# One inference step of a hybrid encoder on one core: VectorE's waits for itself, the spreading of expert ids, and the one-hot tables

## What is computed

```python
x = x + concat([sparse_attention(h), retention(h)]) @ w_out     # h = rmsnorm(x)
x = x + peer(rmsnorm(x));  y = rmsnorm(x)

def peer(h, w_query, keys1, keys2, exp_u, exp_v):               # 8 heads, 128 keys, 16384 experts
    q = (h @ w_query).reshape(T, 8, 2, 128)
    v1, i1 = top_k(q[:, :, 0] @ keys1.T, 16);  v2, i2 = top_k(q[:, :, 1] @ keys2.T, 16)
    cand_s = v1[..., :, None] + v2[..., None, :]                # 256 candidates per head
    top_s, sel = top_k(cand_s, 16);  e_idx = (i1 * 128 + i2)[sel]
    gate = softmax(top_s)
    act = gelu(einsum('thkd,td->thk', exp_u[e_idx], h))
    return einsum('thk,thkd->td', gate * act, exp_v[e_idx])
```

## Time and profile before

| | |
|---|---|
| median of 3 runs | 1158.07 us (1157.69 to 1158.08) |
| profiled execution, its own time | 1156.52 us |
| span of the profile | 1154.5 us |
| busy: PE, DVE, ACT, POOL | 873.4, 816.6, 448.7, 544.4 us |
| mean granted TensorE clock | 0.882 of full |
| bytes moved | 458.68 MB, 397 GB/s over the span |
| chain that ended last | DMA 43%, PE 25%, DVE 17%, POOL 6%, issue 5% |

### The profile page before, as it was taken

One profiled execution on the slowest core, in us unless ns is written; L12 is line 12 of the kernel. 1 busy time (PEld: TensorE's weight loads), 2 busy tenths in 40 slices (PEclk: granted clock), 3 DMA queues, 4 the chain that ended last, 5 costly groups with the idle time before them and its releaser, 6 DMA issues.

```text
span 1154.5 us, 12183 instructions
## 1 busy us (share of the span) xinstructions
PE 873.4 (76%) x3735; PEld 396.8 (34%) x3740; DVE 816.6 (71%) x2123; ACT 448.7 (39%) x1413; POOL 544.4 (47%) x437
## 2 busy tenths in 40 slices
PE   8999988997897957765766769587666756656566
PEld 6748743443333424232233333133222212211111
DVE  2325887876687889996867785757887777777544
ACT  2121444343444434433554663343333333333334
POOL 0002445553554645554553563545574555556442
PEclk9999999999998879787899898798988698887769
DMA  9902999999999999999999999999999999999995
GB/s 377 402 1 72 423 425 425 426 426 430 423 390 425 422 429 425 382 424 425 427 426 424 425 427 427 427 426 428 426 424 426 427 426 427 427 423 418 426 426 226
DMA packets 67079, 458.68 MB, mean 397 GB/s; under 512 B 8387, under 2 KB 10179, under 8 KB 15686
## 3 DMA queue, kind: packets, MB, share of 16 engines
q0 software_dynamic: 55888, 402.68, 83.2%
q1 hardware_dynamic: 10982, 54.97, 11.7%
q10 hardware_dynamic: 144, 0.26, 0.1%
HBM read 453.59 MB, written 3.24 MB: 396 GB/s over the span
## 4 chain that ended last, share of the span: by engine, by line
DMA 43%; PE 25%; DVE 17%; POOL 6%; issue 5%; ACT 3%; SPq 0%; POOLq 0%; DVEq 0%
DMA rows<-in_uv,ids 32%; PE ps L596 25%; DMA wt<-in_uv,ids 8%; DVE rows L2007 7%; POOL rows L535 3%; POOL work L518 2%; DMA rows<-in_w_qi 1%; DMA wt<-in_uv,last_ids 1%; DMA wt<-in_w_q 1%; DVE wt L2007 1%; DVE top L1596 1%; ACT work L1227 1%; DVE wt L1600 1%; ACT wt L1227 1%; POOL wt L535 1%
## 5 line engine op out<-in xcount | busy, mean ns | idle before, releaser
L535 POOL DMA_INDIRECT rows<-in_uv,ids x352 | 407.5, 1158 | 447.6 <-PE ps L596 360.4
L596 PE MATMUL ps<-rows,work 128*64 128x512 f32 x1416 | 419.5, 722 | 236.0 <-ACT work L1227 235.8
L2007 DVE CUSTOM_DVE_ANT_0 rows<-rows,wt 128x1024 f32<-128x1024 f32 x226 | 276.9, 1226 | 150.7 <-DMA rows<-in_uv,ids 147.5
L1227 ACT ACTIVATE zact<-zdot 128x1 f32<-128x1 f32 x354 | 71.5, 202 | 510.1 <-DVE zdot L2007 509.9
L596 PEld LDWEIGHTS ps<-rows,work 128*64 128x64 f32 x1416 | 97.4, 154 | 475.2 <-ACT work L1227 329.4
L596 PE MATMUL ps<-wt 128*128 128x128 f32 (+6 forms) x719 | 195.6, 478 | 27.8 <-ACT wt L1227 26.0
L2007 DVE CUSTOM_DVE_ANT_0 rows<-rows,masks 128x1024 f32<-128x1024 f32 x128 | 157.4, 1232 | 55.7 <-DMA rows<-in_uv,ids 53.1
L596 PEld LDWEIGHTS ps<-wt 128*128 128x128 f32 (+2 forms) x724 | 97.9, 187 | 105.9 <-issue 59.3
L1227 ACT ACTIVATE work<-pair,wgt 128x64 f32<-128x64 f32 x354 | 123.1, 348 | 11.5
L1227 ACT ACTIVATE wgt<-zact,gates 128x1 f32<-128x1 f32 x354 | 104.3, 295 | 11.5
L596 PEld LDWEIGHTS ps<-work,wt 128*128 128x128 f32 (+1 forms) x664 | 85.7, 204 | 55.1 <-issue 55.1
(11 more groups left out here) (175 smaller groups left out, 744.8 us busy)
## 6 DMA issues: line engine op xcount, KB each, us to landing
wt<-in_w_q SPq DMA_DIRECT2D x8, 2048.0 KB, 12.2
rows<-in_uv,ids POOLq DMA_INDIRECT x352, 13.9
rows<-in_w_out SPq DMA_DIRECT2D x2, 2048.0 KB, 31.8
wt<-in_w_out SPq DMA_DIRECT2D x2, 2048.0 KB, 11.3
wt<-in_ckv SPq DMA_DIRECT2D x16, 256.0 KB, 10.8
x<-in_x SPq DMA_DIRECT2D x5, 512.0 KB, 9.0
rows<-in_w_qi SPq DMA_DIRECT2D x1, 2048.0 KB, 13.4
wt<-in_w_qa SPq DMA_DIRECT2D x1, 2048.0 KB, 11.3
```

The source lines that it names most:

```text
L535: pool.indirect_dma_start(row[s], None, a["uv"], bass.IndirectOffsetOnAxis(ap=ids[:, own(n // KP).start + n % KP:own(n // KP).start + n % ...
L596: return nc.tensor.matmul(out, lhsT, rhs, start=start, stop=stop)
L1227: return nc.scalar.activation(*args, **kw)
L2007: V.tensor_tensor_reduce(row[s][:, 0:D], row[s][:, 0:D], h2r[t][:, n % 2, :], 1.0, 0.0, ALU.mult, ALU.add, zdots[s]).then_inc(dotted, 1)
```

## The change

1. A new helper `across` counts the semaphore up, yields, and waits only when the generator is resumed, so behind the dot. The steps of `top16_*`, of the index scoring (`score_round`), of `row_max` and `scale_probs` use it. Where the generator is run through at once (`whole`), the wait comes at once as before.
2. The table `side`, its load and the tile `spread` are gone. TensorE spreads with four matmuls of 64 columns of the identity: half j of the tokens goes to the partitions of q, with the ids and gates that q wants. VectorE takes the result with two copies of 128 partitions.
3. One instruction makes both one-hot tables. The ids' instruction stands ahead of the sum of the exponentials, with no wait of its own, and `flat` has two buffers.
4. Three waits for events of the unit before are added to keep the order: `chosen` and `gexp` in `top16_halves` (the latter was in `top16_pairs`), `picked` in `spread_take`.

```diff
+            def across(ins, s=chain):
+                key = s.name
+                count[key] = n = count.get(key, 0) + 1
+                ins.then_inc(s, 1)
+                yield
+                dve.wait_ge(s, n)
...
-                mm(spread_psum(u), pair[:], spread.rearrange("p j e k -> p (j e k)")).then_inc(spread_ps, 1)
+                for j in range(2):
+                    r = slice(64 * j, 64 * j + 64)
+                    for q in range(2):
+                        last = mm(spread_psum(u)[64 * q:64 * q + 64, j * KP:(j + 1) * KP], ident[:, r],
+                                  flat[u % 2].rearrange("p e (c q) -> p e q c", q=2)[:, :, q, :])
+                last.then_inc(spread_ps, 1)
...
             def score_round(score, r, k, part):
...
-                    then(V.match_replace(out=score, in_to_replace=top8[:], in_values=score, imm_value=TAKEN))
+                    ins = V.match_replace(out=score, in_to_replace=top8[:], in_values=score, imm_value=TAKEN)
+                yield from across(ins)
...
             def top16_halves(u):
                 for e in range(2):
+                    if u >= 1 and e == 1:
+                        dve.wait_ge(chosen, u)
                     ins = V.max(out=top[:, e, 0:8], in_=s[e])
-                then(ins)
-                yield
+                yield from across(ins)
...
             def top16_ids(u):
...
-                for e in range(2):
-                    ins = (V.tensor_tensor(hot[:, e, :, :], rankf[:, e, :]..., iota[:]..., ALU.is_equal))
-                then(ins)
-                yield
-                then(V.tensor_tensor(hot, hot, topf..., ALU.mult))
-                yield
-                then(V.tensor_reduce(half_id, hot, AX.X, ALU.add))
-                yield
+                yield from across(V.tensor_tensor(hot, rankf..., iota[:]..., ALU.is_equal))
+                yield from across(V.tensor_tensor(hot, hot, topf..., ALU.mult))
+                yield from across(V.tensor_reduce(half_id, hot, AX.X, ALU.add))
+                V.scalar_tensor_tensor(flat[u % 2][:, 0, :], half_id[:, 0, :], float(NK), half_id[:, 1, :], ALU.mult, ALU.add).then_inc(chain, 1)
+                count[chain.name] += 1
                 dve.wait_ge(gexp, u + 1)
                 then(V.tensor_reduce(gsum[:], ebest[:, u % 2, :], AX.X, ALU.add))
                 then(V.reciprocal(rgsum[:], gsum[:]))
-                V.tensor_scalar(flat[:, 1, :], ebest[:, u % 2, :], rgsum[:], None, ALU.mult)
-                then(V.scalar_tensor_tensor(flat[:, 0, :], half_id[:, 0, :], float(NK), half_id[:, 1, :], ALU.mult, ALU.add))
+                V.tensor_scalar(flat[u % 2][:, 1, :], ebest[:, u % 2, :], rgsum[:], None, ALU.mult).then_inc(chosen, 1)
                 yield
-                for j in range(2):
-                    ins = V.tensor_scalar(spread[:, j, :, :], flat, side[:, j:j + 1], None, ALU.mult)
-                then(ins, chosen)
 
             def spread_take(u):
                 dve.wait_ge(spread_ps, u + 1)
-                for q in range(2):
-                    r = slice(64 * q, 64 * q + 64)
-                    src = spread_psum(u)[r, :].rearrange("p (j e c q) -> p e q c j", j=2, e=2, q=2)
-                    V.tensor_copy(ids[r, own(u)]..., src[:, 0, q, :, :])
-                    ins = V.tensor_copy(gates[r, own(u)]..., src[:, 1, q, :, :])
-                then(ins, picked)
+                src = spread_psum(u).rearrange("p (j e c) -> p e c j", j=2, e=2)
+                V.tensor_copy(ids[:, own(u)]..., src[:, 0, :, :])
+                if u >= 1:
+                    dve.wait_ge(picked, u)
+                V.tensor_copy(gates[:, own(u)]..., src[:, 1, :, :]).then_inc(picked, 1)
```

More of the change, by code:

```diff
@@ L252, in build @@
                               for i, tile in enumerate((zdot, zact, wgt)))
-        spread = at(work, 3712, 2 * 2 * KP).rearrange("p (j e k) -> p j e k", j=2, e=2)
-        flat = at(work, 3776, 2 * KP).rearrange("p (e k) -> p e k", e=2)
+        flat = [at(work, 3712 + i * 2 * KP, 2 * KP).rearrange("p (e k) -> p e k", e=2) for i in range(2)]
         top = at(work, 3936, 32).rearrange("p (e k) -> p e k", e=2)
@@ L374, in spread_psum @@
         def spread_psum(u):
-            return ps[:, 5 if u else 4, 256:320]
+            return ps[:, 5 if u else 4, 256:256 + 2 * KP]
         def own(u):
@@ L403, in _ @@
             sp.dma_start(x[:, 2, :], a["x"][2]).then_inc(x_in[2], 16)
-            for name, dst in (("e8", e8), ("bar", bar), ("pair", pair[:]), ("side", side[:]), ("m16", m16[:]),
+            for name, dst in (("e8", e8), ("bar", bar), ("pair", pair[:]), ("m16", m16[:]),
                               ("iota", iota[:]), ("kd", kd[:]), ("cs", at(masks, 1536, 384)), ("dmask", at(masks, 0, 1024))):
@@ L1612, in row_max @@
                     dve.wait_ge(expd, step)
[L1613 removed]
+                yield from across(V.tensor_scalar(negmax[:, c:c + w], rowmax[:, c:c + w], -(DH ** -0.5), None, ALU.mult), smax)
             def scale_probs(step, prob, c, w):
@@ L1678, in top16_halves @@
                 for e in range(2):
+                    if u >= 1 and e == 1:
+                        dve.wait_ge(chosen, u)
                     ins = V.max(out=top[:, e, 0:8], in_=s[e])
-                then(ins)
-                yield
+                yield from across(ins)
                 for e in range(2):
                     ins = V.match_replace(out=rest[e], in_to_replace=top[:, e, 0:8], in_values=s[e], imm_value=TAKEN)
-                then(ins)
-                yield
+                yield from across(ins)
                 for e in range(2):
                     ins = V.max(out=top[:, e, 8:16], in_=rest[e])
-                then(ins)
-                yield
+                yield from across(ins)
                 for e in range(2):
                     ins = V.max_index(topi[:, e, 0:8], top[:, e, 0:8], s[e])
-                then(ins, topped)
-                yield
+                yield from across(ins, topped)
                 for e in range(2):
+                    if u >= 1 and e == 1:
+                        dve.wait_ge(gexp, u)
                     ins = V.max_index(topi[:, e, 8:16], top[:, e, 8:16], rest[e])
-                then(ins)
-                yield
+                yield from across(ins)
             def top16_pairs(u):
@@ L1702, in top16_pairs @@
                 c4 = cand.rearrange("p (i j) -> p i j", i=KP)
[L1703 to L1707, removed]
+                yield from across(V.tensor_tensor(c4, top[:, 0, :].rearrange("p (i a) -> p i a", a=1).broadcast_to([P, KP, KP]),
+                                                  top[:, 1:2, :].broadcast_to([P, KP, KP]), ALU.add))
                 then(V.max(out=best[:, 0:8], in_=cand))
-                then(V.match_replace(out=cand2, in_to_replace=best[:, 0:8], in_values=cand, imm_value=TAKEN))
-                yield
+                yield from across(V.match_replace(out=cand2, in_to_replace=best[:, 0:8], in_values=cand, imm_value=TAKEN))
                 then(V.max(out=best[:, 8:16], in_=cand2))
                 if u < HP:
-                    then(V.tensor_scalar(below[:], best, best[:, 0:1], rstd[:, H2_STAT[0]:H2_STAT[0] + 1],
-                                         ALU.subtract, ALU.mult), best_set)
-                else:
-                    then(V.tensor_scalar(below[:], best, best[:, 0:1], None, ALU.subtract), best_set)
-                yield
+                    ins = V.tensor_scalar(below[:], best, best[:, 0:1], rstd[:, H2_STAT[0]:H2_STAT[0] + 1],
+                                          ALU.subtract, ALU.mult)
+                else:
+                    ins = V.tensor_scalar(below[:], best, best[:, 0:1], None, ALU.subtract)
+                yield from across(ins, best_set)
                 V.max_index(besti[:, 0:8], best[:, 0:8], cand)
-                then(V.max_index(besti[:, 8:16], best[:, 8:16], cand2))
-                yield
+                yield from across(V.max_index(besti[:, 8:16], best[:, 8:16], cand2))
             def top16_ids(u):
@@ L1836, in _ @@
             for r in range(0, TOPK[1], 8):
-                score_round(score1, r, TOPK[1], 0)
-                score_round(score1, r, TOPK[1], 1)
+                whole(score_round(score1, r, TOPK[1], 0))
+                whole(score_round(score1, r, TOPK[1], 1))
             set_bias(bias1, score1)
@@ L1861, in attention_1 @@
                 yield from until(8)
-                row_max(1, [ps[:, b, :].rearrange("p (j n) -> p j n", j=2) for b in (1, 2)], 0, 4)
+                yield from row_max(1, [ps[:, b, :].rearrange("p (j n) -> p j n", j=2) for b in (1, 2)], 0, 4)
                 yield from until(10)
-                row_max(2, [ps[:, b, :].rearrange("p (j n) -> p j n", j=2) for b in (0, 3)], 4, 4)
+                yield from row_max(2, [ps[:, b, :].rearrange("p (j n) -> p j n", j=2) for b in (0, 3)], 4, 4)
                 yield from until(15)
-                scale_probs(1, prob1[:, 0, :, :], 0, 4)
-                yield
```

(7 more changed lines are left out.)

47 lines of the change are left out of this document (23 added, 24 removed).

## The result

The changed kernel takes 1170.74 us (median of 5 runs, 1170.42 to 1171.63), the one before 1158.07 beside it (5 runs, 1156.52 to 1158.36): a ratio of 1.0118, 95% interval [1.0104, 1.0132]. It is 12.7 us slower where 1.1 us faster was forecast. The profiled execution has a span of 1168.5 us.

The account below looks back on a forecast made before the run. The DMA engines' transfers were taken as the bound; -0.30 (head), -0.80 (at 470), 0 (at 335) and 0 (tail) sum to -1.10 us, from 1158.07 to 1157.0 us, range 1155.2 to 1159.4.

Parts of the forecast that it names:

- the third stage: The window of 1022 us from 113 to 1135 us, DMA share 1.01: a faster VectorE wins at most about 1.75 us.
- fuller ring: Rival for 400 to 520 us: more gathers in flight raise the rate from 415 to 427 GB/s, 3.4 us won, 1154.4 us; chance 0.12.
- one issue less on SP's queue: At the start, without the load of `side`, later weight loads start a little sooner; put at nothing.
- The rival that ended on the slower side: TensorE becomes the bound up to 350 us, six units at 0.66 us, +4.0 us: 1161.0 us; chance 0.08.
- The head: Everything up to the first gather at 110.63 us: -0.30 us in sum, between -0.50 and -0.10.
- Tables and signal: In unit 0's choice, one table instruction and a shorter chain to TensorE's signal: 0.49 us saved.
- Copies to the gather: In unit 0's choice, two full-height copies instead of four: 0.26 us for 0.53, 0.27 saved.
- TensorE, from its first weight load to the first copy: Spreading before the first gather, six further pairs of weight load and matmul: +0.46 us, between +0.26 and +0.66.
- Worth of a moved wait: On VectorE, a wait moved behind the dot gives about 0.11 us, 34 us of its time in all.
- The 51 us of the forecast: VectorE's time saved over the kernel: 34 us by moved waits, 17 us by removed instructions and shorter tables and copies.
- The dry spot at 470: At 470 to 480 us, DMA engines dry for 0.8 us; the change wins all of it, bounds -0.8 and -0.34.
- At 335: At 335 to 350 us, 0.95 us dry, the late gather waiting for TensorE: 0 won, bounds -0.95 and +0.66.

Follow-up runs that it names:

- a1_pad: The changed kernel plus an unused tile of 8 bytes per partition where `side` stood, restoring the later tiles' SBUF places: 1152.14 us, ratio 0.9963 to the kernel before.
- a2_shift: The kernel before with `side` allocated last, so the row buffers and all that follows lie 32 bytes lower: 1176.49 us, ratio 1.0172 to the kernel before.
- c3_four: a1_pad with the spreading's eight pairs of weight load and matmul done four times over, 24 more a unit: 1152.44 us, ratio 0.9963 to the kernel before.
- b2_no_move: a1_pad with every moved wait put back in front of the dot, the rest of the change kept: 1153.50 us, ratio 0.9967 to the kernel before.
- b1_waits: The kernel before with the moved waits alone; spreading, tables and SBUF places as before: 1153.81 us, ratio 0.9971 to the kernel before.

## Why the prediction was wrong, step by step

**The step that failed** is the limit it set on all effects of the third stage: "All that any speedup of VectorE can win between 113 and 1135 us is about 1.75 us, if the rate of a full DMA stays as it is." The condition was stated and then priced in one direction only (a fuller ring, with more row buffers in flight, raises the rate), never for what the change itself could do to the rate. The removal of `side` was costed as one issue less on SP's queue and put at nothing. It is also an allocation less, ahead of the row buffers and slots into which 400 MB are gathered, and that is the whole of the +18 us: a1_pad undoes it by an unused tile, a2_shift makes it without the change. Why a misplaced packet gets slower stays open. In a kernel whose DMA engines are full for 1022 of 1154 us, 1.5% of their time per packet is 15 us.

**The rival that ended on the slower side** named TensorE. c3_four refutes it: 24 further pairs a unit, four times the six that the change adds, leave the time where it was. That the time came out slower does not make that rival right.

**The head** was right in the size of two terms and too careful in one. Tables and signal: 2.89 us from the tables' start to the signal, 3.39 before, 0.50 won (forecast 0.49). Copies to the gather: 0.55 for 0.83, 0.28 won (0.27). TensorE, from its first weight load to the first copy: 0.46 for 0.54, so 0.08 won, where 0.46 was to be lost and 0.26 at the least. A pair with 64 weight columns and 16 moving ones takes 0.34 / 8 = 0.042 us, the low end of my range and less than the 53 ns estimated there for its weight load alone. The term counted only how long the pairs hold the queue, 0.34 us for 0.22, and left out the time from there to the copy, which fell from 0.32 to 0.12 us. That the last matmul, with 16 moving columns instead of 64, is the reason is likely and not shown. The head gives -0.85 us against -0.30.

**Worth of a moved wait**: 0.11 us, as read. VectorE's busy time fell by 33 us (816.6 to 783.2): 20 us go with the removed instructions alone (796.9 in b2_no_move), 14 with the moved waits alone (802.5 in b1_waits). The 51 us of the forecast held idle time too, so the two can't be set against each other.

**The dry spot at 470** was right as a place and too small as a term. It was counted as dry time only. Around a dry spot there are slow packets as well: of the 8 KB packets of the kernel before, 283 took over 400 ns, 7.1 us above 309 ns by engine; in a1_pad 234, 4.9 us. Of these 2.2 us 1.3 lie at this spot, where the moved waits win 2 us in all for the 0.8 of the forecast. (Its lower bound of 0.34 also left out the 0.42 of L1744, which falls away in each unit.) The rival of the fuller ring had the mechanism right: the rate from 400 to 520 us, 415 GB/s before, is 423 in a1_pad and 427 in c3_four, by its own formula 2.3 and 3.4 us, and its chance of 0.12 was low. It takes the moved waits: b2_no_move has 412 there. The waits alone have 418 in their profiled execution.

```profile
400.00:520.00 120.00, 85.34 (x404) 38.74 (x402) 105.10 (x266) 51.05 (x181) 65.95 (x53) 0.84 1.01 423
```

```profile
400.00:520.00 120.00, 83.66 (x469) 38.60 (x466) 104.07 (x266) 50.33 (x179) 65.10 (x51) 0.84 1.01 427
```

**At 335** the gap stayed, as said: in a1_pad the shares there are still 0.84, 0.98 and 0.99.

Equal places would have given 1158.07 x 0.9963 = 1153.8 us, still 1.4 under the stated range. Of these 4.3 us the head has 0.85 and the spot at 470 some 2; the rest, over 1 us, is not placed.

## What to carry to other kernels

When a change removes or adds a tile, look at the addresses of all that are allocated behind it, above all of the buffers that the bulk of the transfers fills, and keep these at multiples of 256 bytes (shown here for packets of 8 and 16 KB). If a slower run shows the same DMA share at a lower rate, compare the packets' durations before looking at any engine. Where transfers are the bound, a stall can cost more than its dry time (here 2 us for 0.8), and edits that fill the same gap need not add up.

## What the hardware showed that was not expected

In the median a packet of 8192 bytes took 309 ns at a destination on a multiple of 256 bytes, 312 at one 64 or 128 off, and 313 at one 32 or 224 off; but the first 128 packets of 16 KB took 611 ns each, and the first gathers' nearly all 309 ns, wherever they went. An fp32 pair of weight load and matmul with 64 weight columns and 16 moving ones took 0.042 us in a row of eight and 0.032 in one of 32. Both GpSimd's indirect transfers (309 to 313 ns for 8 KB) and the hardware queue's (611 to 614 for 16 KB) are affected. Around the spot at 470 us, where the share fell to 0.92, single packets of 8 KB took up to 1.8 us.
